# Weight slabs split into four places, and token-tile-major first slabs behind the norms of a two-block transformer kernel

## The chip, the core and the metric

The kernel runs on one core of a Trainium2 chip. The core has the engines PE (TensorE: matmuls), DVE (VectorE), ACT (ScalarE), POOL (GpSimd) and SP (queues transfers), and 16 DMA engines. Each engine runs its own instructions in order and they meet in semaphores. The metric is the device time of one execution in microseconds; lower is better.

## The reference

The input is one sequence of 256 tokens of width 1024, all in float32. The first part has two layers. With `mod = silu(c) @ ada_w[l] + ada_b[l]`, split into six rows (shift, scale and gate for attention and for the FFN), a layer is

```
h = rms_norm(x, norm_g[l, 0]) * (1 + sc_a) + sh_a
x = x + g_a * rms_norm(attention(h), norm_g[l, 1])      # plain causal in layer 0, differential in layer 1
h = rms_norm(x, norm_g[l, 2]) * (1 + sc_f) + sh_f
x = x + g_f * rms_norm((silu(h @ w_gate) * (h @ w_up)) @ w_out, norm_g[l, 3])   # hidden width 2816
```

The second part is a mixer (`w_in`; windowed sums, a short convolution and a linear recurrence; `w_out`), an MLP of hidden width 4096 with a squared relu, a gated projection of a second input `p`, and a final norm.

## The kernel before

**Weights as slabs.** All large weights pass as 145 slabs of 1 MB, in one fixed order: `raw` (128 x 2048 float32) is loaded by SP, ACT rounds it to `w_hi` (`split_hi`, L903), DVE forms the rest `w_lo = raw - w_hi` (`split_lo`, L1238), and PE multiplies with both: `three` (L507 to L509) issues hi*hi, hi*lo and lo*hi. `raw`, `w_hi` and `w_lo` each have RING = 3 places. So `split_hi(n)` waits until PE is done with slab n-3 (`slab_done`), and the load of n waits for `split_lo(n-3)`.

**Kinds of slab.** A column slab (`col_slab`, `v_slab`) holds all 1024 rows and 256 columns of a weight; its 48 matmuls have the weights as the stationary operand and 256 tokens (all of them) as the moving one, or the other way round. A row slab (`row_slab`, `row_last_two`) holds 256 rows and 1024 columns: 24 matmuls with 512 moving columns. Layer l has four head pairs of three column slabs (queries, keys, values), four row slabs of `w_o` (OPROJ), then eleven FFN chunks of two column slabs (gate, up) and one row slab (down). Layer 0 starts at slab 0, its FFN at 16; layer 1 at 49, its FFN at 65. The mixer, the MLP and the gate slabs (PLE_GATE) follow.

**Norms.** Behind the last row slab of attention (b = 0, 2) and of the first FFN (b = 1) the functions `post_norm` on ACT and DVE run over two token tiles of 128: square sums of y, x update, square sums of x, `1/rms`, a diagonal matrix of it (`x_diagonal`, L1311), `turn_normed` on PE (x times that matrix, which turns and scales it, L595, with bf16 `keep_warm` matmuls between), the modulation by gain and shift (`t_modulated`, L1326, all on DVE), `hi_part` (L935) and `lo_part` (L1338). The next `col_slab` needs h of all 256 tokens (`Z_NEED`).

**Modulations.** `ada_w` is 48 loads of 1 MB, each summed by DVE in two steps (`ada`, L1246 and L1250). The first 8 come by SP, 40 by POOL's queue (`load_ada`, L465) through three places of `ada_raw`. In layer 0's attention each head pair consumes three; the four of layer 0's FFN gate (items 20 to 23) come around the first norm, in layer 0's FFN four are consumed per two chunks, and the last four in layer 1's attention. Sums become rows by `spread_row` (float32 matmuls with ones, L580) for `gate_row` and columns by `reduce_mods` and `reduce_tile`.

**Order.** The order on every engine is written out by hand. On ACT and DVE each `split_hi` and `split_lo` has its place between the other steps; in a head pair DVE also does `biased` (L1416 to L1435), `normalised` (L1440 to L1462) and ACT the exponentials (`exps`, L983, L985).

Of the kernel before, what the change touches and what calls it, by code (L numbers as in the profile page):

```python
# [7 lines left out]
F32 = mybir.dt.float32  # L8
# [34 lines left out]
RING = 3  # L43
# [17 lines left out]
SH_A, SC_A, G_A, SH_F, SC_F, G_F = range(6)  # L61
ADA_RING = 3

LATER_MODS = (SH_A, SC_A, SH_F, SC_F, G_A)
# [6 lines left out]
OP_ACC = [sorted({0, 1, 2, 4, 7} - {(a + 3 * PAIRS - 1) % RING}) for a in ATTN]  # L71
# [3 lines left out]
TURN = [[4, 5, 6, 7], [2, 3, 5, 6], [0, 2, 4, 5], [0, 3, 5, 6], [0, 1, 4, 5], [1, 2, 4, 5], [4, 5, 6, 7]]  # L75

WARM = {1: 0, 2: 3, 3: 1}
# [3 lines left out]
Z_NEED = [(2, 4)] + [(3, 4)] * 6  # L81
# [10 lines left out]

class Slab:


    def __init__(self, first, stride=0, i=0):
        self.first, self.stride, self.i = first, stride, i

    def __add__(self, k):
        return Slab(self.first + k, self.stride, self.i)  # L100
# [5 lines left out]
    @property  # L106
    def turn(self):
        return self.first // RING + (self.stride // RING) * self.i if self.stride else self.first // RING

    def plus(self, k):  # L110
        return self.first + k + self.stride * self.i if self.stride else self.first + k
# [22 lines left out]
def build(nc, x, c, rel_bias, ada_w, ada_b, norm_g, moba_w_qkv, moba_w_o, diff_w_qkv, diff_w_o, diff_lambda,  # L134
# [8 lines left out]
    with ExitStack() as ctx:  # L143
# [6 lines left out]
        raw = sb("raw", [P, RING, SLAB])  # L150
        w_hi = sb("w_hi", [P, RING, SLAB], F32R)
        w_lo = sb("w_lo", [P, RING, SLAB], F32R)
        ada_raw = sb("ada_raw", [P, ADA_RING, 2, D])
# [5 lines left out]

        junk_x = sb("junk_x", [P, 2, HALF_D])  # L160
# [10 lines left out]
        bias = sb("bias", [P, HEADS, LINE])  # L171
# [6 lines left out]
        ones_r = sb("ones_r", [P, 2], F32R)  # L178
# [3 lines left out]
        c_pair = sb("c_pair", [P, 2])  # L182
# [32 lines left out]
        junk_y = [t[:].rearrange("p a b -> p (a b)") for t in (silu_g, hid)]  # L215
# [8 lines left out]


# [6 lines left out]
        xb, gate_r, gate_i, a_t, th, mult = (view(n) for n in range(6))  # L232
# [3 lines left out]
        pool_d = bias_flat[:, 2 * CT * S:3 * CT * S].rearrange("p (t s) -> p t s", t=CT)  # L236
# [22 lines left out]
        def h_part(h, t, c):  # L259
            return h[:, 4 * c:4 * c + 4, tokens(t)]  # L260

        slab_loaded = [sem(f"slab_loaded_{i}") for i in range(RING)]
        slab_hi, slab_lo, slab_done = sem("slab_hi"), sem("slab_lo"), sem("slab_done")
        first_mods = [sem(f"first_mods_{i}") for i in range(6)]
# [3 lines left out]
        c_pair_ready = sem("c_pair_ready")  # L268
# [14 lines left out]
        diag_ready, turned, t_ready, hi_ready, h_ready = (  # L283
            sem(n) for n in ("diag_ready", "turned", "t_ready", "hi_ready", "h_ready"))
# [28 lines left out]
        def first_mod_place(m):  # L313

            if 3 <= m < 6:
                return raw[:, m - 3].rearrange("p (k n) -> p k n", k=2), first_mods[m % 6]
            return ada_raw[:, (m + 1) % ADA_RING], first_mods[m % 6]
# [30 lines left out]
        def _(sp):  # L348
            def load(n, src, parts):

                if n.stride or n.first >= RING:
                    sp.wait_ge(slab_lo, n.plus(1 - RING))
                else:
                    sp.wait_ge(ada_acc, 2 * (n.first + 4))
                sp.dma_start(parts(raw[:, n.place]), src).then_inc(slab_loaded[n.place], 16)

            def load_gate_rows(b):
# [3 lines left out]
                sp.wait_ge(h_ready, 4 * (b + 1))  # L361
                if b:
                    sp.wait_ge(y_gained, 4 * b)
# [8 lines left out]
            def first_mod(m):  # L372
                buffer, done = first_mod_place(m)
                if m >= 6:
                    sp.wait_ge(ada_acc, 2 * (m - 5))
                sp.dma_start(buffer, rows(ada_w[0][:, ds(m // 4 * D, D)], m % 4)).then_inc(done, 16)
# [22 lines left out]
            for l in range(DEPTH):  # L399
                for t in range(3):  # L400
                    load(Slab(ATTN[l] + t), cols(w_qkv[l], t * D), as_cols)
                with sp.Fori(1, PAIRS) as j:
                    for t in range(3):
                        load(Slab(ATTN[l] + t, 3, j), cols(w_qkv[l], j * 256 + t * D), as_cols)
                load_gate_rows(2 * l)
                for j in range(KT // 2):
                    load(Slab(OPROJ[l] + j), rows(w_o[l], j), as_rows)
                load(Slab(FFN[l]), cols(ffn_w_in[l], 0), as_cols)
                load(Slab(FFN[l] + 1), cols(ffn_w_in[l], D_FF), as_cols)

                def load_chunk(n, j):
# [3 lines left out]

                with sp.Fori(0, FF_CHUNKS - 3) as j:
                    load_chunk(Slab(FFN[l] + 2, 3, j), j)
                load_gate_rows(2 * l + 1)
                for j in (FF_CHUNKS - 3, FF_CHUNKS - 2):
                    load_chunk(Slab(FFN[l] + 2 + 3 * j), j)  # L420
# [19 lines left out]
            sp.wait_ge(y_gained, 4 * 4)  # L440
            sp.dma_start(grow[:], on_all(norm_final_g_2, 0)).then_inc(final_row_loaded, 16)
            load(Slab(MLP), cols(w_up_2[0], 0), as_cols)
            with sp.Fori(0, (UP_CHUNKS - 1) // 3) as i:
                for c3 in range(3):
                    n = Slab(MLP + 1 + 2 * c3, 6, i)
                    load(n, cols(w_up_2[0], i * 768 + 256 * (c3 + 1)), as_cols)
                    load(n + 1, rows(w_down_2[0], i * 3 + c3), as_rows)
            sp.wait_ge(mix_ready, 2)
# [12 lines left out]
        def _(pool):  # L461
            def load_ada(l, kp, col, place, need):

                pool.wait_ge(ada_acc, need)
                pool.dma_start(ada_raw[:, place], rows(ada_w[l][:, ds(col, D)], kp)).then_inc(ada_loaded[place], 16)  # L465
# [1469 lines left out]
```

## Time and profile before

| | before |
|---|---|
| median of 3 runs | 1021.24 us (1018.68 to 1021.3) |
| the profiled execution's own time | 1020.94 us |
| its span | 1019.2 us |
| PE, DVE, ACT busy | 940.8, 683.6, 471.7 us |
| DMA | 213 MB, 209 GB/s over the span |

The span is the time from the first to the last instruction of the profiled execution. Matmuls are pipelined, so a busy matmul shows a length of its own, and the distance of two starts is what it costs.

### The profile page before, as it was taken

The numbers are of one execution on the slowest core, as the hardware profiler recorded it, in microseconds if no ns is written. First come the engines' busy times: TensorE is split into PE (matmuls) and PEld (weight loads), VectorE is DVE, ScalarE is ACT, GpSimd is POOL, SyncE is SP. The second block draws the span as 40 slices with busy tenths as digits, with TensorE's granted clock in tenths as the row PEclk, the third lists the DMA queues.
The fourth block names the chain that finished last, engine by engine and source line by source line (L and its number), as shares of the span: only waits on it lengthen the run. The fifth ranks groups of instructions, "written<-read, shape, count | busy, mean of one in ns | idle before, by whom it ended". The sixth has DMA issues, their size and how long they took to land.

```text
span 1019.2 us, 15585 instructions
## 1 busy us (share of the span) xinstructions
PE 940.8 (92%) x6301; PEld 861.1 (84%) x6301; DVE 683.6 (67%) x793; ACT 471.7 (46%) x599; POOL 37.3 (4%) x93
## 2 busy tenths in 40 slices
PE   1699998999999989999899999997997999999985
PEld 1699977999999979997789999996986999999864
DVE  5788877968767778887754444456895554555555
ACT  2254445434334345766554343434483544354553
POOL 2101100100000000000000000000000000000000
PEclk9799999999999999999999999998999999999988
DMA  8999960989779645655245556662444656665511
GB/s 336 369 329 325 342 227 36 356 296 338 272 268 364 233 151 165 207 209 170 75 165 176 196 174 214 200 217 92 143 152 139 197 175 193 181 203 187 178 69 41
DMA packets 127840, 213.00 MB, mean 209 GB/s; under 512 B 4673, under 2 KB 97970, under 8 KB 127794
## 3 DMA queue, kind: packets, MB, share of 16 engines
q1 hardware_dynamic: 116466, 168.82, 49.6%
q0 software_dynamic: 11328, 43.53, 11.6%
q8 instruction: 33, 0.54, 0.2%
q14 instruction: 13, 0.11, 0.0%
HBM read 211.28 MB, written 1.06 MB: 208 GB/s over the span
## 4 chain that ended last, share of the span: by engine, by line
PE 79%; DVE 9%; ACT 5%; DMA 4%; issue 2%; SPq 0%; DVEq 0%; ACTq 0%
PE ps L507 25%; PE ps L509 24%; PE ps L508 24%; DMA raw<-in_moba_w_qkv 3%; DVE w_lo L1238 2%; ACT w_hi L903 2%; DMA ada_raw<-in_ada_w 1%; DVE yg L1326 1%; DVE ada_sum L1250 1%; PE ps L694 1%; PE ps L580 1%; PE ps L595 1%; DVE h_lo L1338 1%; DVE yg L1333 1%; ACT h_hi L935 1%
## 5 line engine op out<-in xcount | busy, mean ns | idle before, releaser
L1238 DVE TENSOR_TENSOR w_lo<-raw,w_hi 128x2048 fp32r<-128x2048 f32 x145 | 331.8, 2290 | 202.5 <-ACT w_hi L903 202.3
L903 ACT ACTIVATE w_hi<-raw 128x2048 fp32r<-128x2048 f32 x145 | 276.7, 1910 | 245.3 <-PE ps L509 227.2
L507 PE MATMUL ps<-h_hi,w_hi 128*128 128x256 f32 x1312 | 376.9, 287 | 11.5 <-DVE h_lo L1338 9.7
L508 PE MATMUL ps<-h_lo,w_hi 128*128 128x256 f32 x1312 | 374.5, 285 | 0.0
L509 PE MATMUL ps<-h_hi,w_lo 128*128 128x256 f32 x1312 | 374.3, 285 | 0.0
L507 PEld LDWEIGHTS ps<-h_hi,w_hi 128*128 128x128 f32 x1312 | 255.2, 194 | 15.3 <-issue 11.4
L508 PEld LDWEIGHTS ps<-h_lo,w_hi 128*128 128x128 f32 x1312 | 255.2, 194 | 1.2
L509 PEld LDWEIGHTS ps<-h_hi,w_lo 128*128 128x128 f32 x1312 | 255.1, 194 | 0.0
L507 PE MATMUL ps<-w_hi,o_hi 128*128 128x512 f32 x264 | 106.0, 402 | 4.7 <-issue 1.7
L509 PE MATMUL ps<-w_hi,o_lo 128*128 128x512 f32 x264 | 103.5, 392 | 0.0
L508 PE MATMUL ps<-w_lo,o_hi 128*128 128x512 f32 x264 | 103.5, 392 | 0.0
L1250 DVE SCALAR_TENSOR_TENSOR ada_sum<-ada_raw,c_act,ada_sum 128x1024 f32<-128x1024 f32 x51 | 65.4, 1282 | 4.4 <-DMA ada_raw<-in_ada_w 3.2
L507 PEld LDWEIGHTS ps<-w_hi,o_hi 128*128 128x128 f32 x264 | 50.1, 190 | 15.5 <-issue 3.8
L509 PEld LDWEIGHTS ps<-w_hi,o_lo 128*128 128x128 f32 x264 | 49.8, 189 | 10.9
L508 PEld LDWEIGHTS ps<-w_lo,o_hi 128*128 128x128 f32 x264 | 50.1, 190 | 9.1
L507 PE MATMUL ps<-w_hi,hid_hi 128*128 128x512 f32 x144 | 57.1, 397 | 0.1
L507 PE MATMUL ps<-w_hi,h_hi 128*128 128x256 f32 (+1 forms) x160 | 50.9, 318 | 6.4 <-DVE w_lo L1238 5.4
L508 PE MATMUL ps<-w_lo,hid_hi 128*128 128x512 f32 x144 | 56.2, 390 | 0.0
L509 PE MATMUL ps<-w_hi,hid_lo 128*128 128x512 f32 x144 | 56.0, 389 | 0.0
L508 PE MATMUL ps<-w_lo,h_hi 128*128 128x256 f32 (+1 forms) x160 | 49.8, 311 | 0.0
L509 PE MATMUL ps<-w_hi,h_lo 128*128 128x256 f32 (+1 forms) x160 | 49.6, 310 | 0.0
L1054 ACT ACTIVATE silu_g<-ps 128x512 f32<-128x512 f32 x22 | 13.1, 596 | 78.3 <-PE ps L509 78.3
(241 smaller groups left out, 964.5 us busy)
## 6 DMA issues: line engine op xcount, KB each, us to landing
raw<-in_ffn_w_in SPq DMA_DIRECT2D x44, 1024.0 KB, 5.2
ada_raw<-in_ada_w POOLq DMA_DIRECT2D x40, 1024.0 KB, 7.5
raw<-in_ffn_w_out SPq DMA_DIRECT2D x22, 1024.0 KB, 5.0
raw<-in_w_up SPq DMA_DIRECT2D x16, 1024.0 KB, 5.7
raw<-in_w_down SPq DMA_DIRECT2D x16, 1024.0 KB, 4.9
raw<-in_moba_w_qkv SPq DMA_DIRECT2D x12, 1024.0 KB, 8.5
raw<-in_diff_w_qkv SPq DMA_DIRECT2D x12, 1024.0 KB, 5.2
raw<-in_w_in SPq DMA_DIRECT2D x6, 1024.0 KB, 5.1
```

The costliest lines, as they stand in the source:

```text
L507: T.matmul(out_ap, hi_s, hi_m, start=start, stop=False, skip_group_check=True)
L508: T.matmul(out_ap, hi_s, lo_m, start=False, stop=False, skip_group_check=True)
L509: return T.matmul(out_ap, lo_s, hi_m, start=False, stop=stop, skip_group_check=True)
L580: last = T.matmul(ps[:, banks[c]], ones[:], ada_sum[:, slot, half(c)], start=True, stop=True)
L595: last = T.matmul(ps[:, TURN[z][2 * t + c], f * P:(f + 1) * P], xt[:, t, fs], diag[:, t], start=True, stop=True)
L694: T.matmul(late, q[rs, hh, P:S], k[rs, hh, :], start=True, stop=True)
L903: A.activation(w_hi[:, n.place], raw[:, n.place], ACT.Copy).then_inc(slab_hi, 1)
L935: A.activation(h_part(h_hi, t, c), turned_tile(t, c), ACT.Copy).then_inc(hi_ready, 1)
L1054: A.activation(silu_g[:], ps[:, n.place], ACT.Silu).then_inc(silu_ready, 1)
L1238: V.tensor_tensor(w_lo[:, n.place], raw[:, n.place], w_hi[:, n.place].bitcast(F32), ALU.subtract).then_inc(slab_lo, 1)
L1250: V.scalar_tensor_tensor(out=ada_sum[:, slot], in0=buffer[:, k], scalar=scalars[k], in1=ada_sum[:, slot], op0=ALU.mult, op1=ALU.add)\
L1326: last = V.tensor_scalar(turned_tile(t, c)[:, f], ps[:, TURN[z][2 * t + c], f * P:(f + 1) * P], gains[:, k:k + 1], mods[:, shift, k:k + 1] ...
```

## The change

- `w_hi` and `w_lo` have four places, `raw` keeps three (RAW = 3, RING = 4). `split_hi(n)` waits for the end of slab n-4, and nearly every split on ACT and DVE is of the slab after the one that it was (n+3 for n+2, and so on). PSUM banks go by `first % 3` as before. Room comes from `bias` (256 columns instead of 384), `junk_x` (gone), the third place of `ada_raw` (now `yg`) and views laid over others.
- Behind the three norms with modulation the first two slabs are half-row slabs (`load_two`: 512 rows, 256 columns each of gate and up, or of queries and keys). `first_two` multiplies them token tile by token tile, 512 moving columns at a time. Results have tokens as rows: `hidden_tokens` and `tokens_out` bring them to SBUF, and transposes turn the hidden chunk (4) or queries and keys (8).
- x is scaled by DVE (`xs_ready`) and transposed, instead of multiplied by a diagonal; tile 1's transposes stand within `first_two`. Half of `t_modulated` is on ACT.
- `spread_row` takes sums that are split into hi and lo (`gate_hi`, `gate_lo`), two float32r matmuls for one float32 matmul.
- Items of `ada_w` have a new order (`ADA`): layer 0's FFN gate is summed in layer 0's FFN, five items per two chunks; two of layer 1's attention gate in layer 1's attention; layer 1's FFN gate in its FFN. Places are held until the h of a norm is ready.
- Layer 1's `lambda_and_decay` moves behind the first split of its attention. Loops over chunks and pairs are written out (no `Fori`).

The core of the diff:

```diff
-RING = 3
+RAW = 3
+RING = 4
-LATER_MODS = (SH_A, SC_A, SH_F, SC_F, G_A)
+LATER_MODS = (SH_A, SC_A, SH_F, SC_F)
...
+            def first_two(n, z, banks, turn_second):
+                for t in range(ST):
+                    for s in range(2):
+                        if t == 0:
+                            pe.wait_ge(slab_lo, n.plus(s + 1))
+                        pe.wait_ge(h_ready, 4 * z + 2 * t + s + 1)
+                        wh, wl = as_halves(w_hi[:, (n + s).place]), as_halves(w_lo[:, (n + s).place])
+                        for k in range(4):
+                            if (t, s, k) == (0, 1, 2):
+                                turn_second()
+                            kk = 4 * s + k
+                            last = three(ps[:, banks[t]], h_hi[:, kk, tokens(t)], h_lo[:, kk, tokens(t)],
+                                         wh[:, k], wl[:, k], kk == 0, kk == KT - 1)
+                        if t == 1:
+                            last.then_inc(slab_done, 1)
+                    if t == 0:
+                        last.then_inc(first_done, 1)
...
+                pe.wait_ge(gate_lo_ready, b + 1)
+                hi, lo = gate_split(b)
                 for c in range(2):
-                    last = T.matmul(ps[:, banks[c]], ones[:], ada_sum[:, slot, half(c)], start=True, stop=True)
+                    T.matmul(ps[:, banks[c]], ones_r[:], hi[:, half(c)], start=True, stop=False, skip_group_check=True)
+                    last = T.matmul(ps[:, banks[c]], ones_r[:], lo[:, half(c)], start=False, stop=True,
+                                    skip_group_check=True)
...
+                    if l and first:                                  # PE, first pair of layer 1
+                        first_two(n, 2, QK_TOKENS, lambda: turn_second(2))
+                        v_slab(n + 2, {1: turn_queries_keys, 5: lambda: scores(pairs * 3 + 2)})
+                        return
...
+                    if l and first:                                  # ACT, first pair of layer 1
+                        tokens_out(n, QK_TOKENS, 0)
+                        split_hi(n + 3)
+                        tokens_out(n, QK_TOKENS, 1)
+                        split_hi(n + 4)
+                        act.wait_ge(tok_turned, 2)
+                        queries_out(ps[:, QK_TURNED[0]])
+                        A.activation(qkv[:, 1], ps[:, QK_TURNED[1]], ACT.Copy).then_inc(qkv_out, 1)
+                        values_out(n + 2)
+                        exps(pairs + 1)
+                        split_hi(n + 5)
+                        return
...
+                    if first:                                        # DVE, a head pair
+                        split_lo(n + 2)
+                    if l == 0:
+                        ada(FIRST_MODS + 3 * j)
+                    elif first:
+                        lambda_and_decay()
                     split_lo(n + 3)
+                    if l == 0:
+                        ada(FIRST_MODS + 3 * j + 1)
+                    elif j < 2:
+                        ada(ADA_GA + 2 + j)
+                    if l and first:
+                        split_lo(n + 4)
                     if l:
                         biased(pairs + 1, 2 * j)
...
+                    if l and first:
+                        split_lo(n + 5)
                     normalised(pairs + 1, j + 1)
...
+                gate_lo(2 * l)                                       # DVE, before w_o; gate_hi stands so on ACT
                 split_lo(n + 3)
```

## Rows read from the trace of the kernel before

**Rows 1.** The page: its head and the engines' busy time.

```profile
span 1019.2 us, 15585 instructions
...
PE 940.8 (92%) x6301; PEld 861.1 (84%) x6301; DVE 683.6 (67%) x793; ACT 471.7 (46%) x599; POOL 37.3 (4%) x93
```

**Rows 2.** Timeline of PE, from a row slab to a column slab: start, length.

```profile
542.05 0.39 PE L509 MATMUL ps<-w_hi,hid_lo 128*128 128x512 f32 x1
542.28 0.28 PE L507 MATMUL ps<-h_hi,w_hi 128*128 128x256 f32 x1
...
542.51 0.28 PE L509 MATMUL ps<-h_hi,w_lo 128*128 128x256 f32 x1
```

**Rows 3.** Stretches: length, busy time of each engine, PE's clock, DMA share, GB/s.

```profile
56.00:127.00 71.00, 70.14 (x558) 68.29 (x556) 63.07 (x70) 33.66 (x51) 7.74 (x11) 1.00 0.93 333
...
214.00:362.00 148.00, 147.42 (x1035) 137.59 (x1036) 106.71 (x81) 57.70 (x44) 9.86 (x14) 1.00 0.81 286
...
703.00:720.00 17.00, 10.57 (x61) 9.96 (x60) 11.77 (x24) 10.31 (x20) 0.00 (x0) 0.70 0.11 35
```

**Rows 4.** Groups of instructions: busy us, mean ns, idle time before them.

```profile
L1238 DVE TENSOR_TENSOR w_lo<-raw,w_hi 128x2048 fp32r<-128x2048 f32 x145 | 331.8, 2290 | 202.5 <-ACT w_hi L903 202.3
L903 ACT ACTIVATE w_hi<-raw 128x2048 fp32r<-128x2048 f32 x145 | 276.7, 1910 | 245.3 <-PE ps L509 227.2 <-DMA raw<-in_moba_w_qkv 18.1
...
L1250 DVE SCALAR_TENSOR_TENSOR ada_sum<-ada_raw,c_act,ada_sum 128x1024 f32<-128x1024 f32 x51 | 65.4, 1282 | 4.4 <-DMA ada_raw<-in_ada_w 3.2
...
L1326 DVE TENSOR_SCALAR yg<-ps,gain,mods 128x128 f32<-128x128 f32 x64 | 21.7, 402 | 3.6 <-PE ps L595 3.6
...
L1338 DVE TENSOR_TENSOR h_lo<-yg,h_hi 128x512 fp32r<-128x512 f32 x28 | 19.1, 688 | 7.7 <-ACT h_hi L935 7.1
...
L935 ACT ACTIVATE h_hi<-yg 128x512 fp32r<-128x512 f32 x28 | 17.4, 629 | 54.1 <-DVE yg L1333 29.4 <-DVE yg L1326 24.7
...
L985 ACT ACTIVATE prob<-prob,maxes 128x128 f32<-128x128 f32 x24 | 9.3, 387 | 0.0
```

**Rows 5.** The chain of waits around layer 0's first norm: start, length, what.

```profile
134.93 1.98 PE ps L580 x4
...
159.82 0.91 PE ps L595 x8
...
185.03 0.39 PE ps L507
```

**Rows 6.** The chain of waits at the start of layer 1's attention.

```profile
396.50 0.61 ACT qkv L1023
```

**Rows 7.** Timeline of DVE, ACT and PE in layer 1's first head pair.

```profile
400.09 0.42 DVE L1423 TENSOR_TENSOR prob<-ps,bias 128x256 f32<-128x256 f32 x1
...
404.38 0.51 ACT L983 ACTIVATE prob<-prob,maxes 128x256 f32<-128x256 f32 x1 [5.49 <-DVE maxes L1435]
...
409.58 1.41 DVE L1462 SCALAR_TENSOR_TENSOR prob<-prob,rsums 128x256 f32<-128x256 f32 x4
...
416.13 0.27 PE L646 MATMUL ps<-ident,prob 128*128 128x128 f32 x1
```

**Rows 8.** The chain of waits around layer 1's FFN norm.

```profile
477.78 3.64 PE ps L580 x4
...
499.64 0.91 PE ps L595 x8
...
525.20 0.38 PE ps L507
```

**Rows 9.** PE's waits from 480 to 800 us: us in total, times, longest.

```profile
PE ps L507 <- DVE w_lo L1238: 2.6, 2, 1.5
```

**Rows 10.** Timeline of PE at the gate slabs, the kernel's end.

```profile
987.21 0.79 PE L507 MATMUL ps<-w_hi,h_hi 128*128 128x512 f32 x1 [2.74 <-DVE w_lo L1238]
...
998.53 0.47 PE L507 MATMUL ps<-w_hi,h_hi 128*128 128x512 f32 x1 [2.71 <-DVE w_lo L1238]
```

**Rows 11.** Timeline of ACT at the kernel's start.

```profile
57.36 1.91 ACT L903 ACTIVATE w_hi<-raw 128x2048 fp32r<-128x2048 f32 x1 [0.34 <-DMA raw<-in_moba_w_qkv]
```

More of the change, by code:

```diff
@@ L710, in pair @@
                         turn_heads(j)
-                pair(0, Slab(ATTN[l]), True)
-                with pe.Fori(1, PAIRS) as j:
-                    pair(j, Slab(ATTN[l], 3, j), False)
+                for j in range(PAIRS):
+                    pair(j, Slab(ATTN[l] + 3 * j), j == 0)
                 pairs = PAIRS * (l + 1)
@@ new lines, in _ @@
+                last.then_inc(tok_turned, 1)
+                col_slab(n + 1, None, FF_UP[l])
+                down(n + 2, base + 1, 0)
+                for chunk in range(2, FF_CHUNKS - 1):
+                    n = Slab(FFN[l] + 3 * chunk - 1)
+                    gate_up(n, base + chunk)
+                    if chunk == FF_CHUNKS - 2:
+                        pe.wait_ge(mod_ready, 8)
+                        spread_row((FF_FREE[l], MISC), 2 * l + 1)
+                    turns = l == 0 and chunk % 2 == 0
+                    if turns:
+                        i = chunk // 2 - 1
+                        pe.wait_ge(ada_lo_ready, i + 1)
+                        pe.wait_ge(mod_ready, i + 4)
+                    down(n + 2, base + chunk, (chunk - 1) % 2, reduce_tile if turns else None)
@@ L840, in up_down @@
                 row_slab(n + 1, FF_ACC, hidden_parts(parts), False)
-            with pe.Fori(0, (UP_CHUNKS - 4) // 3) as i:
-                for c3 in range(3):
-                    up_down(Slab(MLP + 1 + 2 * c3, 6, i), i * 3 + (c3 + 1), c3)
+            for chunk in range(UP_CHUNKS - 4):
+                up_down(Slab(MLP + 1 + 2 * chunk), chunk + 1, chunk % 3)
             for o in range(2):
@@ new lines, in _ @@
+                hidden_tokens(1)
+                split_lo(n + 4)
+                dve.wait_ge(hid_hi_ready, base + 1)
+                V.tensor_tensor(hidden_parts(0)[1], ps[:, MISC].rearrange("p (o s) -> p o s", o=2),
+                                hidden_parts(0)[0].bitcast(F32), ALU.subtract).then_inc(hid_lo_ready, 1)
+                for chunk in range(1, FF_CHUNKS):
+                    n = Slab(FFN[l] + 3 * chunk - 1)
+                    last, even = chunk == FF_CHUNKS - 1, chunk % 2 == 0
+                    i = (chunk - 1) // 2
+                    m = ADA_LATER + 5 * i
+                    if last:
+                        gate_row(2 * l + 1, (FF_FREE[l], MISC), (9, 11)[l])
+                    split_lo(n + 3)
+                    if l == 0 and not last:
+                        ada(m + (3 if even else 0))
+                    if l and chunk <= KT // 2:
+                        ada(ADA_GF + chunk - 1)
+                    if not last:
+                        split_lo(n + 4)
+                    if chunk == FF_CHUNKS - 2:
+                        gate_lo(2 * l + 1)
+                    if l == 0 and not last:
@@ L1865, in _ @@
             x_scaled(0)
-            split_lo(n)
+            split_lo(n + 1)
             x_scaled(1)
```

778 lines of the change are left out of this document (384 added, 394 removed).

## The prediction

> **What bounds the kernel now.** I read the page first: PE is busy for 940.8 of 1019.2 us, DVE for 683.6 [rows 1]. A busy matmul overlaps the next, so I took PE's cost from distances of starts: one with 512 moving columns takes 0.23 us, two with 256 take 0.23, so 0.12 each (the finer value is 0.1195) [rows 2]. A row slab of 24 is then 5.5 us, a column slab of 48 is 5.75 us, and 145 slabs are some 820 us. Then the stretches: in layer 0's attention after the start (56 to 127 us) and in its FFN (214 to 362 us) PE is idle for 0.9 and 0.6 us at full clock, with the DMA queues at 333 and 286 GB/s [rows 3]. These stretches, which with the second layer's and the MLP are most of the time, are bound by PE, and an earlier split gives nothing there. ACT's 245 us and DVE's 202 us of idle time before the splits are mostly waits for PE through the three places [rows 4]; they matter only where PE then waits for a split. What is left to win lies between the stretches: the start, the three norms with modulation, the mixer and the gate slabs at the end. I read the chain of waits and PE's timeline there.
>
> **Layer 0's FFN norm.** The last slab of w_o ends at 159.82; PE starts the third FFN slab (the first of the second chunk) at 185.03 [rows 5]. That is 25.2 us, of which the two slabs are 11.5. New order, counted from 159.82: the transposes of tile 0's first half take 0.45 (half of the 0.91 of the eight float32 passes [rows 5]). DVE modulates one quarter in 4 instructions, some 1.4 us at the 0.34 between overlapped starts behind the 402 ns [rows 4]. ACT can start its own quarter 1.2 behind 159.82, after the last square sum. The trace before has no modulation on ACT. Its price: below, four times the 0.29 between starts of a 128-column exponential with one per-partition operand (387 ns long [rows 4]), 1.3 us; above, four times 0.6 (the length of a 512-column h_hi, 629 ns), 2.4 us. It is nearest to the 128-column row, with a second operand that adds some 0.09: I take 1.6. Then two h_hi (0.63, the second 0.53 later) and an h_lo (0.69) [rows 4]: PE starts at +3.9. Twelve matmuls 2.75, six 1.35, tile 1's transposes 0.9 (its x update, square sums, root and two scalings end at about +7.6, in time for them), six more 1.35: +10.3. Tile 1's quarters then take 1.6 + 0.6 + 0.7 behind their transposes at +9.0, so PE waits until +11.9, and 24 matmuls (5.5) end at +17.3. ACT's table load and split of the third slab and DVE's split (1.3 + 1.9 + 2.3) end at the same time. So 17.3 for 25.2, less 0.45 for the four transposes of the hidden chunk: 7.4 us saved.
>
> The row of ones costs 1.98 at 134.93 [rows 5]; four float32r matmuls cost 0.91, and `gate_lo` is ready in time, because ACT and DVE run one slab ahead: 1.0 saved. PE's wait for the biased scores of 0.7 us at 127 goes too, as DVE no longer waits there for w_hi. Against it stands DVE's queue in the first two FFN chunks: five sums of 2.5 us per two chunks instead of four, 6 splits of 2.2, hidden 2 x 1.2 and the split of the column sums 1.2 are 30 of 36.3 us, so the stretch stays PE's, but it begins late: from +19.1 (DVE) split, sum, split, sum, split, sum ... I count `hidden` of chunk 2 at 0.8 us and the split of the sums of the next chunk at 2.0 us after PE wants them; from chunk 4 on the queue has caught up. Loss 2.8 (bounds 0 and 5). Sum for this place: 7.4 + 1.0 + 0.7 - 2.8 = 6.3 us. DMA in this FFN goes from 10 to 11 MB per 36.3 us, 318 GB/s, under the 333 at which the attention stretch kept PE busy [rows 3].
>
> The Trainium skill speaks against this step: "ScalarE: Activation LUTs", section "What ACT_TABLE_LOAD costs", has 186 ns plus 0.833 ns per element and 93 ns for each per-partition operand, overlapped by 93. By it the four modulations are an estimated 1.6 us, and the sum is the same; by the lower bound above it would be 0.6 us per norm better.
>
> **Layer 1's attention (second norm).** PE's part is as above: the first two slabs end some 7 us earlier than now, when the last key left ACT at 397.1 [rows 6], and queries and keys are turned inside the value slab. But DVE's order behind them is split, `lambda_and_decay` 3.3, split, sum 2.5, split, and only then `biased`: it starts at about 399.5 against 400.09 now [rows 7], one split more ahead of it than before. From its start 4.3 to the exponentials (404.38), 3.5 more for them [rows 7]; then ACT splits slab n+5 (1.9), DVE splits it (2.3 [rows 4]) and only then normalises (2.9, ending now at 411.0 [rows 7]). Ready: 399.5 + 4.3 + 3.5 + 1.9 + 2.3 + 2.9 = 414.4. PE has finished the next queries and keys by 409 (now at 416.13 [rows 7]) and turns the probabilities only then: a stall of some 5.4 us takes the place of the one removed. A stall of 2.74 us before the end was followed by a spell at half clock: 24 matmuls that take 5.5 took 8.6 [rows 10]. I put 2 us for it here. Gain of this place 7 - 5.4 - 2 = 0 (bounds -3 and +7: if DVE got through earlier, all of it stays). The row of ones in chunk 9 gives 0.7.
>
> **Layer 1's FFN norm.** As layer 0's, 499.64 to 525.20 now, 25.6 us [rows 8]. Here ACT and DVE must do two splits between the last head and the norm, where one stood: DVE enters the norm 2.7 us later, of which 2.2 reach PE. `gate_lo` stands behind the normalisation and a split, at 480.0, while PE is ready at 477.78; the four matmuls then take 1.8 at half clock instead of 3.64 [rows 8]: 0.4 lost. So 25.6 - 17.3 - 0.45 - 2.2 - 0.4 = 5.2 saved, and 0.8 for the row of ones in that FFN: 6.0.
>
> **Mixer.** PE waited twice for a split between 480 and 800 us, 2.6 us in all, 1.5 at the last two slabs of w_out [rows 9]. That split now stands ahead of the recurrence's last steps: 1.5 saved.
>
> **Gate slabs.** PE waits 2.74 and 2.71 us for splits [rows 10], the second slab runs 3.1 us slow. With one more slab split ahead the second slab's halves are there at 972, and the last two at 991.35, while PE arrives at 990.0. PE's last 11.2 us start at 991.4 instead of 998.53: 7.1 saved. The work behind it is the same.
>
> **Start.** Keys now leave ACT behind the split of slab 4, which before came after them, at 57.36 and waiting for its load [rows 11]. Its load competes with 1.5 MB less from POOL's queue (bias 1.0 for 1.5 MB, the third sum's load held back). I take a loss of 0.7 (bounds -2 and +2). Loops written out, the missing copies of `c_pair`, and `clear_acc` cost or give nothing: PE shows no gap at a loop's turn, and the clear lay in a wait. If instruction fetch lost this cover, it would be the pauses of a rival, not of the sum.
>
> **Sum.** 6.3 + 0.7 + 6.0 + 1.5 + 7.1 - 0.7 = 20.9 us. The profiled execution took 1020.94 us (span 1019.2), 0.3 under the median of 1021.24: 1000.0 us. A measurement tells 0.3%, some 3 us, from no change.
>
> **Rivals.**
> - *No stall in layer 1's first pair.* For it: biased scores may start sooner, each of the five steps is short. Against: all are in DVE's written order. Gives 7 more: 993. Chance 0.17.
> - *The clock falls at each norm.* PE's transposes replace products with a diagonal, and only 8 keep-warm matmuls are left. For it: in the fourth norm, which turns by transposes and has a 5 us wait, the stretch 703 to 720 has a clock of 0.70 [rows 3]. Against: the new waits of PE are under 2 us. A half-clock slab costs 2.5 to 3 us, three times: 1008. The skill's "TensorE: Matmul & The Clock Gate", Part 4, says that transposes do not count as busy for the clock, which would bring this about; no row before parts transposes from waits. Chance 0.15.
> - *The end gives nothing*, as the load of the last slabs or ACT becomes late: 7.1 less, 1007. Against: these loads have 10 us of room. Chance 0.07.
> - *Slower: layer 0's FFN is bound by the sums.* The fifth load per two chunks comes late, and DVE waits in order, with splits behind it. It decides from 4.7 us per two chunks over 4.5 such periods (21 us), that is, if 11.5 MB take 41 us, 280 GB/s. 286 GB/s took a share of 0.81 [rows 3], so some 350 are to be had. At 43 us the result is 1030. Chance 0.06.
> - *No change worth measuring*: new waits in the norms (ACT's share of the modulation at 2.4 us, DVE late) eat all: 1019. Chance 0.05.
>
> **How the numbers follow.** The forecast has the remaining 0.50, with its own range of 994 to 1006. Faster by over 0.3%: 0.50 + 0.17 + 0.15 + 0.07 = 0.89, same 0.05, slower 0.06. The range 987 to 1010 takes in the first three rivals with their bounds and leaves out the last two and a little below.
>
> **What would show it.** Right: third FFN slab 17 to 18 us behind the last of w_o in both layers; PE idle for 4 to 6 us before the turned probabilities of layer 1's first pair; one wait of 1.4 us instead of two of 2.7 at the gate slabs; DVE waited for in chunks 2 and 3 of layer 0. Wrong: waits for sums in every FFN period, clock under 1 behind each norm, or no stall in layer 1.

## The result and the profile after

The changed kernel takes 1013.17 us (median of 5, 1012.85 to 1014.3) against 1021.24 us (median of 5, 1018.68 to 1023.44): a ratio of 0.9925, 95% interval 0.9912 to 0.9938. It is 8.1 us faster, where 21 were forecast; 1013.17 lies above the range. The profiled execution took 1013.14 us with a span of 1011.3. The head of its page and the engines' busy time, to be held against [rows 1]:

```profile
span 1011.3 us, 14324 instructions
...
PE 919.6 (91%) x6067; PEld 842.1 (83%) x6071; DVE 682.3 (67%) x775; ACT 484.7 (48%) x631; POOL 36.3 (4%) x92
```

PE is busy for 21.2 us less, and the span is 7.9 shorter, so PE's idle time has grown by 13 us; the question is where. The stretches, with the same columns as [rows 3]:

```profile
127.00:160.00 33.00, 32.10 (x164) 27.30 (x163) 21.08 (x31) 15.56 (x28) 0.00 (x0) 0.95 0.60 192
...
178.00:214.00 36.00, 33.51 (x243) 31.38 (x242) 30.58 (x22) 17.07 (x14) 3.51 (x5) 1.00 0.93 337
214.00:362.00 148.00, 139.68 (x983) 130.91 (x982) 109.67 (x88) 55.66 (x42) 11.91 (x17) 0.98 0.86 303
```

Layer 0's FFN, where PE was idle for 0.6 of 148 us [rows 3], now has 8.3 us of idle time. The prediction had called that stretch bound by PE and had expected a gain of 0.7 there. PE's waits of the changed kernel say who is waited for (us in total, times, longest):

```profile
PE ps L682 <- DVE yg L1463: 22.3, 2, 20.2
PE ps L566 <- DVE h_lo L1482: 16.5, 9, 5.8
PE ps L664 <- DVE o_lo L1407: 8.0, 2, 7.7
PE ps L734 <- DVE prob L1635: 5.9, 2, 5.0
...
PE ps L664 <- DVE h_lo L1407: 3.2, 1, 3.2
...
PE ps L782 <- ACT qkv L1183: 2.0, 1, 2.0
```

L682 are the transposes, L664 is the first matmul of the row of ones, L734 turns the probabilities, L782 are the scores. The third and the fifth are new; the fourth was 0.9 us in all before, the last 1.4 in two places.

To see what each part was worth I took the same landmark in both timelines of PE (the start of a given slab, or for w_o its end) and subtracted. A term is the difference of two neighbouring landmarks' lags.

| place | from, to (before; after) | gain | forecast |
|---|---|---|---|
| start to the first scores | 57.07; 59.22 | -2.15 | -0.7 |
| attention of layer 0, its row of ones | to the transposes at 159.66; 160.02 | +1.79 | +1.7 |
| first norm | to the third FFN slab, 185.03; 177.73 | +7.66 | +7.4 |
| first FFN chunks | to the third chunk, 221.35; 216.93 | -2.88 | -2.8 |
| chunks 3 to 8 | to 330.19; 325.82 | -0.05 | 0 |
| row of ones in the ninth chunk | to 348.98; 353.32 | -8.71 | +0.7 |
| second norm | to the slab behind the value slab, 404.61; 402.06 | +6.89 | +7 |
| layer 1's first pair | to the first slab of w_o, 469.38; 474.18 | -7.35 | -7 |
| row of ones, layer 1's attention | to the end of w_o, 499.64; 505.84 | -1.40 | -0.4 |
| third norm | to the third FFN slab, 525.20; 525.92 | +5.48 | +5.6 |
| layer 1's FFN | to 679.85; 680.60 | -0.03 | +0.8 |
| mixer and MLP | to the gate slabs, 978.79; 977.89 | +1.65 | +1.5 |
| gate slabs | to the last two, 998.53; 990.60 | +7.03 | +7.1 |

The gains sum to 7.9, the forecasts to 20.9. (In layer 1's first pair the prediction's own terms, 5.4 and 2, make 7.4; its sum took 7. It booked the transposes of the hidden chunk, 0.45, with the norms; they stand behind that landmark, so in the table 0.35 us of them falls to the row below the first and the third norm.) One term, the row of ones in the ninth chunk, carries 9.4 of the 13.0 us between them; the start 1.5, the row of ones in layer 1's attention 1.0, layer 1's FFN 0.8.

**The place that failed.** Timelines of the changed kernel around it, first SP's DMA issues (start, length):

```profile
305.65 0.37 SPq L411 DMA_DIRECT2D raw<-in_ffn_w_out  x1
325.20 0.34 SPq L428 DMA_DIRECT2D grow<-in_norm_g  x1
325.58 0.43 SPq L429 DMA_DIRECT2D yg<-in_ada_b  x1
326.44 1.01 SPq L411 DMA_DIRECT2D raw<-in_ffn_w_in  x2
```

Then the chain of waits through it (start, length, what):

```profile
326.44 9.15 DMA raw<-in_ffn_w_in
...
335.61 1.92 ACT w_hi L1003
...
337.56 2.29 DVE w_lo L1382
...
343.95 1.23 DVE o_lo L1407
...
345.32 0.77 PE ps L664
```

From 305.65 to 325.20, 19.5 us, SP issues nothing. In its written order it stands at the loads of the gate row for the FFN. One of them goes into `bias_row`, which is `yg[:, 0]`, and the change made `yg` the third buffer for the modulations' parts; so `load_gate_rows` got a wait for the sums (`sp.wait_ge(ada_acc, 2 * 40)` for this row). That sum ends at 325.1 on DVE. Three slab loads stand behind the row in SP's queue and start at 326.4 where the first could have started at some 311. ACT waits 14.8 us for the first of them, and `gate_lo` stands on DVE behind that slab's split, a sum and the next split, although its own input has long been there. PE is ready for the row of ones at 337.58 and gets it at 345.32, and the matmuls behind it start at half clock: the clock of 338 to 352 is 0.76.

**The places that held.** The chain through the first norm, with the columns of [rows 5]:

```profile
160.21 0.70 ACT hid L1010 x2
...
161.20 1.49 ACT yg L1045 x4
162.68 0.53 ACT h_hi L1039
163.23 0.70 DVE h_lo L1482
...
168.44 0.89 PE ps L682 x8
169.35 1.50 ACT yg L1045 x4
170.86 0.53 ACT h_hi L1039
171.41 0.70 DVE h_lo L1482
```

ACT's modulation of a quarter takes 1.50 us (forecast 1.6). PE starts at 164.07, 3.9 us behind the last slab of w_o, and at 177.73 the third slab runs. The gate slabs of PE, against the two waits of [rows 10]:

```profile
977.89 0.47 PE L566 MATMUL ps<-w_hi,h_hi 128*128 128x512 f32 x1 [0.95 <-DVE h_lo L1482]
990.60 0.47 PE L566 MATMUL ps<-w_hi,h_hi 128*128 128x512 f32 x1 [1.58 <-DVE w_lo L1382]
```

And the stall that was forecast in layer 1's first head pair, on DVE, ACT and PE, against [rows 7]:

```profile
411.52 3.70 ACT L1003 ACTIVATE w_hi<-raw 128x2048 fp32r<-128x2048 f32 x2
...
417.40 0.58 ACT L1183 ACTIVATE qkv<-ps 128x512 f32<-128x512 f32 x1
```

```profile
413.45 2.29 DVE L1382 TENSOR_TENSOR w_lo<-raw,w_hi 128x2048 fp32r<-128x2048 f32 x1 [5.49 <-ACT w_hi L1003]
...
417.20 1.41 DVE L1635 SCALAR_TENSOR_TENSOR prob<-prob,rsums 128x256 f32<-128x256 f32 x4
```

```profile
418.75 0.45 PE L734 MATMUL ps<-ident,prob 128*128 128x128 f32 x1 [5.01 <-DVE prob L1635]
```

### The profile page after: what moved, and what is told of

Read it like the earlier page. It is cut to its first block, busy times and chain, and to the rows that moved or that the text cites. A ratio compares the mean times of both kernels' runs of the same rounds, so it can differ in the third digit from the quotient of the medians.

```text
span 1011.3 us, 14324 instructions
## 1 busy us (share of the span) xinstructions
PE 919.6 (91%) x6067; PEld 842.1 (83%) x6071; DVE 682.3 (67%) x775; ACT 484.7 (48%) x631; POOL 36.3 (4%) x92
## 4 chain that ended last, share of the span: by engine, by line
PE 76%; DVE 11%; ACT 5%; issue 3%; DMA 3%; SPq 0%; DVEq 0%; ACTq 0%
PE ps L566 24%; PE ps L568 23%; PE ps L567 23%; DVE w_lo L1382 3%; DVE ada_sum L1400 3%; ACT w_hi L1003 2%; DMA ada_raw<-in_ada_w 1%; DVE h_lo L1482 1%; PE ps L782 1%; DMA raw<-in_ffn_w_in 1%; DMA raw<-in_moba_w_qkv 1%; ACT yg L1045 1%; PE ps L655 1%; ACT h_hi L1039 1%; DVE yg L1477 1%
## 5 line engine op out<-in xcount | busy, mean ns | idle before, releaser
L566 PE MATMUL ps<-h_hi,w_hi 128*128 128x256 f32 x1216 | 348.4, 287 | 10.3 <-DVE h_lo L1482 8.6
L567 PE MATMUL ps<-h_lo,w_hi 128*128 128x256 f32 x1216 | 346.5, 285 | 0.0
L568 PE MATMUL ps<-h_hi,w_lo 128*128 128x256 f32 x1216 | 346.5, 285 | 0.0
L566 PEld LDWEIGHTS ps<-h_hi,w_hi 128*128 128x128 f32 x1216 | 236.0, 194 | 13.2 <-issue 9.4
L567 PEld LDWEIGHTS ps<-h_lo,w_hi 128*128 128x128 f32 x1216 | 236.1, 194 | 1.2
L568 PEld LDWEIGHTS ps<-h_hi,w_lo 128*128 128x128 f32 x1216 | 235.8, 194 | 0.0
L566 PE MATMUL ps<-w_hi,h_hi 128*128 128x256 f32 (+1 forms) x208 | 69.3, 333 | 9.5 <-DVE h_lo L1482 7.9
L567 PE MATMUL ps<-w_lo,h_hi 128*128 128x256 f32 (+1 forms) x208 | 67.4, 324 | 0.0
L568 PE MATMUL ps<-w_hi,h_lo 128*128 128x256 f32 (+1 forms) x208 | 67.4, 324 | 0.0
L566 PEld LDWEIGHTS ps<-w_hi,h_hi 128*128 128x128 f32 x208 | 39.6, 190 | 15.9 <-issue 7.1
```

The source lines that it names most:

```text
L566: T.matmul(out_ap, hi_s, hi_m, start=start, stop=False, skip_group_check=True)
L567: T.matmul(out_ap, hi_s, lo_m, start=False, stop=False, skip_group_check=True)
L568: return T.matmul(out_ap, lo_s, hi_m, start=False, stop=stop, skip_group_check=True)
```

## The experiments

Each run below is the changed kernel with one edit unless it says otherwise. The median is given, and the span of its profiled execution, which compares with 1011.3. Executions whose edit acts only later reach the third FFN slab up to 1.7 us later than the changed kernel's 177.73, so the verdict on an edit is read from its own stretch of PE's timeline.

**e1_rows_later: the gate row's loads one chunk later in SP's queue.**

```diff
-                    if j == FF_CHUNKS - 3:
+                    if j == FF_CHUNKS - 2:
                         load_gate_rows(2 * l + 1)
```

> The changed kernel with one step of SP's queue moved: the loads of the FFN gate row (norm weights and bias row) stand behind the loads of the last but one chunk instead of one chunk earlier; nothing else. Theory A (SP's queue): in the changed kernel these loads wait for the last sum of layer 0 (ended 325.04), because the bias row goes into the buffer that the third sum's loads use, and the three slab loads behind them start at 326.44 instead of some 311; ACT waits 14.8 us for the first of them, gate_lo stands behind that slab's split on DVE, and PE waits 7.74 us. Moved, the slab loads start at about 311, the wait of PE is gone and the stretch from the ninth chunk's first slab to the tenth's falls from 27.5 to about 18 us: 9.5 us less, 1003.7. Theory B (DVE is simply full in this FFN, with five sums per two chunks): the wait only moves to the next splits, under 3 us less, 1010 or more. Theory C (the load itself, 9.15 us where the usual one is 5.4, is slow from contention with POOL's loads): 3 to 4 us less.

1004.48 us (1003.9 to 1005.06), span 1003.3, against the kernel before 0.9834 (0.9799 to 0.9870). SP's issues in this run:

```profile
312.46 6.54 SPq L411 DMA_DIRECT2D raw<-in_ffn_w_in  x2
323.97 0.37 SPq L411 DMA_DIRECT2D raw<-in_ffn_w_out  x1
326.55 0.34 SPq L428 DMA_DIRECT2D grow<-in_norm_g  x1
326.94 0.43 SPq L429 DMA_DIRECT2D yg<-in_ada_b  x1
```

The slab loads go out from 312.5, the gate row's at 326.5, much as before, where nothing urgent stands behind them. The ninth chunk takes 18.5 us instead of 27.5 (327.1 to 345.6), 9.0 less, and PE's wait there is 0.28. (The kernel before needs 18.8, so with the loads out of the way the row of ones gives 0.3 here, not the 0.7 that was forecast.) Theory A holds; DVE has room for its five sums, and the load is not slow by itself.

**e2_ones_ahead: SP's queue as it is, gate_hi and gate_lo ahead of the late splits.**

```diff
-                    split_hi(n + 3)
                     if chunk == FF_CHUNKS - 2:
                         gate_hi(2 * l + 1)
+                    split_hi(n + 3)
...
+                    if chunk == FF_CHUNKS - 2:
+                        gate_lo(2 * l + 1)
                     split_lo(n + 3)
...
-                    if chunk == FF_CHUNKS - 2:
-                        gate_lo(2 * l + 1)
```

> The changed kernel with SP's queue as it is, but in the chunk before the last the two parts of the gate row (gate_hi on ACT, gate_lo on DVE) stand ahead of the splits of that chunk instead of behind them; in both layers. Theory A: slab loads still start at 326.4, but PE no longer waits for gate_lo at 337.6; it does the row of ones and the row slab that is long split until about 344, when the late slabs 29 and 30 are split (339.8 and 344.0). The wait of 7.7 us goes down to at most 2: 6 to 8 us less, 1006. Theory B (the late loads themselves are what PE waits for, wherever gate_lo stands): at most 2 us less, 1011.

1008.92 us (1007.04 to 1013.98), span 1007.5. The row of ones runs at 339.02 without a wait, and then PE waits for `hidden`, which DVE has behind the late splits too:

```profile
348.86 0.58 PE L566 MATMUL ps<-h_hi,w_hi 128*128 128x256 f32 x1 [3.30 <-DVE hid L1720]
```

The ninth chunk takes 21.5 us (327.4 to 348.9), 6.0 less than 27.5. So with the loads late, 6 of the 9 us come through the place of `gate_lo` behind the late split and 3 through what else stands behind it. In the span 3.8 us of it show: this execution is 1.6 us behind already at its third FFN slab, and some 0.7 more are lost behind the tenth chunk's start.

**e3_before_rows_wait: the kernel before, with the wait alone.**

```diff
                 sp.wait_ge(h_ready, 4 * (b + 1))
+                if b == 1:
+                    sp.wait_ge(ada_acc, 2 * 40)
```

> The kernel before with only the wait added: its loads of layer 0's FFN gate row wait for the sum number 40 (the last of chunk 8, ended 318.07). Three slab loads behind them start some 13 us later than now (318 instead of 305). Theory A (a wait in SP's queue costs what the late split then holds up, and here no part of the row of ones stands behind a split): the first late slab is needed at 330.2 and would be split at about 331.5: 1 to 3 us more, 1023. Theory B (the wait alone costs what it cost the changed kernel): 8 to 10 us more, 1030.

1035.89 us (1033.04 to 1037.39), span 1031.3 against 1019.2: 12 us longer in the span, and by the ratio, 1.0149 (1.0112 to 1.0186) of the kernel before, 15 us. From the eighth chunk's first slab to the ninth's PE needs 34.9 us instead of 19.2: the loss in its own stretch is 15.7 us, of which the span shows less, because this execution was 1.7 us ahead at the first norm and wins 2 back in layer 1. Theory A was wrong, and the loss is above B's upper bound. ACT's timeline, and then DVE's and PE's:

```profile
328.99 1.91 ACT L905 ACTIVATE w_hi<-raw 128x2048 fp32r<-128x2048 f32 x1 [13.14 <-DMA raw<-in_ffn_w_in]
```

```profile
330.93 2.29 DVE L1240 TENSOR_TENSOR w_lo<-raw,w_hi 128x2048 fp32r<-128x2048 f32 x1 [14.61 <-ACT w_hi L905]
333.14 1.22 DVE L1597 TENSOR_TENSOR o_lo<-ada_sum,o_hi 128x1024 fp32r<-128x1024 f32 x1
```

```profile
334.41 0.79 PE L509 MATMUL ps<-w_hi,o_hi 128*128 128x512 f32 x1 [13.44 <-DVE o_lo L1597]
```

I had asked when PE needs the late slab (330) and not what stands behind its split on ACT and DVE. `hidden` and the split of the column sums stand there, and PE wants them at 321. A load that is late by 13 us cost 13.44 us of PE's time, though the slab itself had 9 us of room. A late load is late for everything that is written behind its split.

**e4_norm_keys_first and e7_norm_first: the order in layer 1's first pair.** The first has both halves of this edit, the second only DVE's:

```diff
-                    split_hi(n + 3)
+                    if l == 0 or j != 1:
+                        split_hi(n + 3)
                     act.wait_ge(slab_done, n.plus(1))
                     queries_out(ps[:, n.bank])
-                    split_hi(n + 4)
+                    if l == 0 or j != 1:
+                        split_hi(n + 4)
                     act.wait_ge(slab_done, n.plus(2))
                     A.activation(qkv[:, 1], ps[:, (n + 1).bank], ACT.Copy).then_inc(qkv_out, 1)
+                    if l and j == 1:
+                        split_hi(n + 3)
+                        split_hi(n + 4)
...
+                    normalised(pairs + 1, j + 1)
                     if l and first:
                         split_lo(n + 5)
-                    normalised(pairs + 1, j + 1)
```

> The changed kernel; in layer 1's first head pair DVE normalises the probabilities ahead of the split of the slab behind, and in the second pair ACT copies queries and keys out ahead of its two splits. Theory A (the stall of 5.0 us at 418.7 is the split of 2.3 and ACT's split of 1.9 ahead of the normalisation, and then the copies of the keys at 417.4): PE turns the probabilities at about 414.5, the scores follow at 415.2 instead of 420.19: 5 us less, 1008. Theory B (the stall is the biased scores' late start at 403.7, so the order behind the exponentials changes little): under 1.5 us less, 1012.

> Only half of the run before it in layer 1's first pair: DVE normalises ahead of the split, ACT's order stays. Theory A (two waits in a row: probabilities, then keys): the probabilities are turned at 414.5, but the scores wait for ACT's copy of the keys, which ends at 418.0: 2 us less, 1011. Theory B (DVE's order is all of it): as much as both together, 3.7 us less in the span.

Both: 1009.83 us (1009.34 to 1015.86), span 1007.6. DVE's order alone: 1013.28 us (1010.44 to 1016.35), span 1011.5. From the last matmuls of the first pair's value slab to the slabs of the third pair PE needs 30.4 us in the changed kernel, 26.4 with both and 29.6 with DVE's half. PE with both, and with one half:

```profile
414.79 0.30 PE L734 MATMUL ps<-ident,prob 128*128 128x128 f32 x1 [1.01 <-DVE prob L1640]
```

```profile
415.86 0.33 PE L734 MATMUL ps<-ident,prob 128*128 128x128 f32 x1 [2.02 <-ACT qkv L1154]
...
418.14 1.23 PE L782 MATMUL ps<-qkv 64*128 64x256 f32 x4 [1.41 <-ACT qkv L1183]
```

The stall was two waits in one place, DVE's normalisation and ACT's copies of queries and keys behind two splits. Taking one away shows the other: 0.9 us gained (2 were expected; the scores do start 2.05 earlier, but they and the heads' matmuls behind them take 5.6 us instead of 4.6, more of it at half clock). Both together give 4.0 of the 5 expected; PE now waits 1.6 us between the scores and the heads' matmuls.

**e5_late_tail: the gate slabs' splits one step later.** `split_hi` and `split_lo` of the four gate slabs stand at the kernel before's places. This is DVE's part; ACT's is the same with `split_hi`:

```diff
-            split_lo(n + 4)
             dve.wait_ge(p_hi_ready, 1)
...
             x_scaled(0)
-            split_lo(n + 1)
+            split_lo(n)
             x_scaled(1)
...
-            split_lo(n + 2)
+            split_lo(n + 1)
             dve.wait_ge(x_rms, 10)
             V.reciprocal(rsx[:, 6], rmsx[:, 6]).then_inc(x_rstd, 1)
-            split_lo(n + 3)
+            split_lo(n + 2)
...
+                if j == 0:
+                    split_lo(n + 3)
```

> The changed kernel with the splits of the four gate slabs one step later on ACT and DVE, at the places that they have in the kernel before (the last of them behind the first scaled gate); four places stay. Theory A (the 7.0 us of the kernel's end come from the one slab of lead): the two waits of 2.7 us and the half-clock slab come back: 7 us more, 1020. Theory B (they come from something else, such as the earlier loads or the four places themselves): no change, 1013.

1022.76 us (1020.64 to 1026.14), span 1022.0. PE's gate slabs:

```profile
989.24 0.50 PE L566 MATMUL ps<-w_hi,h_hi 128*128 128x512 f32 x1 [2.72 <-DVE w_lo L1383]
...
999.67 0.47 PE L566 MATMUL ps<-w_hi,h_hi 128*128 128x512 f32 x1 [3.07 <-DVE w_lo L1383]
```

The waits of 2.7 us are back, and from the first gate slab to the last PE needs 31.6 us instead of 23.8: 7.8 us for 7 expected. The lead of one slab is what the end gained from. (Of the other 2.9 us of the span 1.7 came in the first 200 us and 0.6 around the ninth chunk.)

**e6_whole_tile: PE waits for the whole of h behind all three norms.**

```diff
+                turn_second()
+                pe.wait_ge(h_ready, 4 * z + 4)
                 for t in range(ST):
                     for s in range(2):
                         if t == 0:
                             pe.wait_ge(slab_lo, n.plus(s + 1))
-                        pe.wait_ge(h_ready, 4 * z + 2 * t + s + 1)
...
-                            if (t, s, k) == (0, 1, 2):
-                                turn_second()
```

> The changed kernel, but PE turns tile 1 before it starts tile 0 of the two half-row slabs and waits for all four quarters of h before the first product, behind all three norms; everything else as it is (modulation halved with ACT, split a slab ahead). Theory A (the gain of 7.5 us at each norm is the overlap of tile 0's products with tile 1's chain): PE starts the two slabs at +11.9 instead of +3.9 and needs 11 us: third slab at +23 instead of +17.7, 5.3 us more at each of three norms, and more where PE's longer idle time is followed by half clock: 1029 to 1035. Theory B (the gain is mostly the halved modulation and the earlier splits): under 2 us at each norm, 1013 to 1019.

1032.75 us (1031.43 to 1034.34), span 1032.4. PE's two waits at the first norm (start, length):

```profile
168.83 1.97 PE L681 MATMUL ps<-ident,yg 128*128 128x128 f32 x8 [4.39 <-DVE yg L1462]
174.24 0.79 PE L566 MATMUL ps<-w_hi,h_hi 128*128 128x512 f32 x1 [3.44 <-DVE h_lo L1481]
```

From the first transpose to the third FFN slab PE needs 25.2 us (161.68 to 186.87) instead of 17.7: 7.5 more where 5.3 were expected, as the two slabs take 12.6 for 11 behind the waits, part of it at half clock. The kernel before needed 25.4 between the same two places. The stretches of the other two norms are 8.1 and 8.0 longer, and layer 1's first pair 3.8 shorter, since DVE has caught up there by the time PE comes. So the gain at a norm is the overlap of tile 0's products with tile 1's chain; where PE waits for all of h, the halved modulation, the transposes for diagonal products and the earlier splits together give 0.2 us.

**e8_start_keys: in layer 0's first pair the keys ahead of the split of slab 4.**

```diff
-                    split_hi(n + 4)
+                    if not (l == 0 and first):
+                        split_hi(n + 4)
                     act.wait_ge(slab_done, n.plus(2))
                     A.activation(qkv[:, 1], ps[:, (n + 1).bank], ACT.Copy).then_inc(qkv_out, 1)
+                    if l == 0 and first:
+                        split_hi(n + 4)
```

> The changed kernel; in layer 0's first pair ACT copies the keys out ahead of the split of slab 4, as the kernel before does. Theory A (PE's wait of 2.05 us for the keys at 59.2 is that split, which waited 4.05 us for its load): the scores start at about 57.9: 1.3 to 2 us less, 1011.5. Theory B (the whole start is late by its loads, and the next wait takes it over): no change.

1013.02 us (1011.77 to 1014.76), span 1011.2: no change. The scores start at 57.99 instead of 59.22, and the lead of 1.2 us holds up to 195.0 (196.2 in the changed kernel). At the next chunk it is gone (216.8 against 216.9), and PE's wait there for the split of the column sums is 2.7 us instead of 1.6. DVE's timeline shows why:

```profile
203.45 2.60 DVE L1403 SCALAR_TENSOR_TENSOR ada_sum<-ada_raw,c_act,ada_sum 128x1024 f32<-128x1024 f32 x2 [0.96 <-DMA ada_raw<-in_ada_w]
```

Between 190 and 220 us the DMA share is 1.0 in both runs: the restarted slab loads and the sums' loads fill the queues. So in this execution theory B holds. It is no rule, though: the combined kernel below has the same edit, comes to this FFN 2.5 us earlier than the changed kernel, has no such wait of DVE, and still has the whole 2.5 us at the third chunk (214.47 for 216.93). Why the load came late in e8 stays open, and so whether the edit is worth 0 or 1.2 us.

**e9_gate_lo_first: in layer 1's attention gate_lo one split earlier.**

```diff
                         heads_low(pairs, heads_before)
+                    if l and j == PAIRS - 1:
+                        gate_lo(2)
                     if not (l and first):
                         split_lo(n + 5)
...
-                gate_lo(2 * l)
+                if l == 0:
+                    gate_lo(0)
                 split_lo(n + 3)
```

> The changed kernel; in layer 1 DVE computes gate_lo for the attention's gate row ahead of the last pair's fifth split instead of behind it. Theory A (PE's wait of 3.21 us at 484.89 and the half clock behind it are that one split of 2.3): gate_lo ends at about 482.5, when the turned probabilities are copied out too, so PE starts the row of ones there: 2.3 us less, and up to 1 more where the clock then stays: 1010.5. Theory B (the late split only moves the wait to the row slabs behind): under 1 us less.

1011.11 us (1010.52 to 1011.32), span 1008.7. PE:

```profile
483.77 0.47 PE L664 MATMUL ps<-h_hi,ones_r 128*128 128x512 f32 x1 [1.01 <-DVE h_lo L1407]
```

The wait falls from 3.21 to 1.01 us, and the four matmuls take their full-clock distance of 0.23 instead of 0.43. The stretch to the FFN's second chunk is 3.9 us shorter (86.8 for 90.7), 2.2 of them the wait and most of the rest time at full clock.

**e10_combined: e1, e4, e8 and e9 in one kernel.** Its diff is theirs.

> All that helped in one kernel: gate row loads later in SP's queue (8.0 less in the span by itself), normalisation and key copies first in layer 1 (3.7), keys ahead of the split of slab 4 in layer 0 (0 to 1.2), gate_lo ahead of the split in layer 1's last pair (2.3 expected). Theory A (the waits are separate stretches, so they add): 8.0 + 3.7 + 2.3 = 14 less, 999. Theory B (what one frees the next wait takes, as the gain at the start was taken up in layer 0's FFN): 10 less, 1003.

994.94 us (993.76 to 997.0, 5 runs), span 991.9; against the kernel before 0.9746 (0.9721 to 0.9771). The span is 19.4 us under the changed kernel's (the medians are 18.2 apart), more than either theory gave. By stretches: ninth chunk 9.0, first pair 4.0, layer 1's row of ones and norm 3.8, which are what each edit gave in its own stretch and add to 16.8, so the waits add, as in theory A; and 2.5 ahead of layer 0's FFN, where its timeline is at 193.7 instead of 196.2. Of these 0.9 are the keys; 1.4 lie where the last two slabs of w_o run:

```profile
127.00:160.00 33.00, 32.05 (x171) 26.70 (x170) 22.54 (x36) 16.82 (x31) 0.00 (x0) 1.00 0.57 192
```

Its clock there is 1.00, where the changed kernel had 0.95 and needed 12.6 us for these two slabs instead of 11.2. Each of the four edits alone left them at 12.6 to 12.8. But e3, whose only edit first acts some 150 us later, took 11.2 there too, where the kernel before has 12.6. So these 1.4 us come and go between executions, and nothing here shows that the four edits together bring them.

## Why the prediction was wrong

The direction and most of its steps were right; the time was not, by 13 us, and one missed wait is over two thirds of that.

- **Row of ones in the ninth chunk of layer 0** ("The row of ones in chunk 9 gives 0.7", "from chunk 4 on the queue has caught up"; measured -8.7). This is the step that failed. The part on this FFN followed DVE's queue and summed up the DMA, and did not read SP's queue past the moved sums: the gate row's loads now wait for the last of them, with three slab loads behind. e1 moves the loads and has 9.0 us back; e2 leaves them and has 6.0 back by taking `gate_lo` out from behind the late split; e3 puts the wait alone into the kernel before and loses 15.7 us in its stretch, 12 in the span. The term was also too large by itself: without the late loads the row of ones gives 0.3 here.
- **Slower rival: layer 0's FFN bound by the sums.** Its pattern was right (a late load, and DVE in order behind it), its mechanism was not: it was one wait in SP's queue of slab loads, 8.7 us, not a period that repeats; from chunk 3 to chunk 8 the changed kernel loses 0.05 us on the one before.
- **Norms** (7.4, 7 and 5.6 forecast; 7.7, 6.9 and 5.5 measured). The chain was right step by step, and e6 shows that it is the overlap that pays: without it the stretch is back at 25.2 us. The third FFN slab starts 17.6 us behind the last of w_o in layer 0, as the forecast's sign has it, but 20.1 behind it in layer 1: the sign left out the 2.2 us by which DVE comes late to that norm, which the sum had; PE waits 2.13 us for it. The Trainium skill's page "ScalarE: Activation LUTs", section "What ACT_TABLE_LOAD costs", gave an estimated 1.6 us for the four modulations; the trace has 1.50.
- **First FFN chunks** (2.8 forecast, 2.9 measured). The waits are where they were forecast, 0.9 us for `hidden` and 1.6 for the split of the column sums. That DVE's order alone sets them was only argued: in e8 a sum waits 0.96 us for its load there, with the DMA share at 1.0.
- **Layer 1's first pair** (stall of 5.4 and 2 of clock forecast; 5.01 measured, 7.35 in all). Right, and incomplete: ACT's copies of queries and keys were the second wait in the same place, which e7 uncovers.
- **Row of ones in layer 1's attention** (0.4 lost forecast, 1.4 measured). `gate_lo` is where it was reckoned (done at 484.75, that is 479.95 on the clock of the kernel before, for "480.0"), and the row of ones costs 0.5 more than before. What was left out are the heads' matmuls behind it, which run at half clock too, 0.9 us. e9 takes 2.2 us of wait away and gains 3.9.
- **Layer 1's FFN** (0.8 forecast, nothing measured). From the last matmul ahead of the row of ones to the slab behind it PE takes 7.0 us (673.58 to 680.60) where it took 7.3 (672.53 to 679.85): 0.3 gained, as in layer 0 without the late loads, because the float32 row of ones costs 1.32 us between starts here (672.65 to 673.97), less than the 1.98 that were read at 134.93. The transposes of the hidden chunk, 0.35, stand in this stretch and take it back.
- **Start** (0.7 lost forecast, 2.15 measured, beyond the bound of 2). The keys wait behind slab 4's split as forecast, with a wait of 2.05 us where there was one of 0.69: ACT waited 4.05 us for that slab's load. The first slab also starts 1.1 later (43.26 for 42.12): the last sum ends 0.9 later, as DVE scales x ahead of it, two times 0.88 us, where it made two diagonals of 0.29, and PE's reduction behind that sum takes 3.54 us for 2.45. Whether the 1.2 us of the keys would have counted in the end is open: e8 paid them back, the combined kernel did not.
- **Gate slabs** (7.1 and 7.0) and **mixer** (1.5 and 1.65) were right; e5 has 7.8 for the first.
- **The clock at each norm.** This rival did not come: the clock from 160 to 178 us is 1.00 (0.91 before), although PE transposes there, and in the second norm (375.9 to 394) it is 1.00 too. In the third (505.8 to 526) it is 0.92, behind the wait of 2.13 us, where the kernel before has 0.93 (499.6 to 525.2). The Trainium skill's page "TensorE: Matmul & The Clock Gate", Part 4, which says that transposes do not count as busy in the same way, is not contradicted by it, as products and keep-warm matmuls stand between them.

## What to carry to other kernels

When a buffer gets a second user, look for every queue in which a wait is written for it, and list what stands behind that wait; a DMA queue counts as one, and here one wait in it cost more than anything else in the change. A late load is late for all that stands behind its split in the order of the splitting engines, so its room is not the time until its own slab is needed but the time until the first of these is. And where two engines feed one place, an experiment that moves only one of them can show nothing while both together pay.

## What the runs showed of the hardware

Layer 0's last two slabs of w_o, which stand behind the 16 one-column float32 matmuls (32 in the trace) that reduce the modulations, took 12.6 to 12.8 us in seven of the twelve profiled executions, 13.7 to 13.9 in three (e2, e5, e6) and 11.2 in two (e3, e10), with the same instructions: part of them at half clock, by an amount that changes. Such spells are why an edit's worth of 1 or 2 us could be read only from its own stretch. A wait of PE of 3.21 us in layer 1 was followed by 3.4 us at half clock (the four matmuls of 512 columns started 0.43 apart); after a wait of 1.01 us in the same place (e9) they started 0.23 apart. The length of the wait alone does not decide it: at the end of the kernel before, the matmuls behind a wait of 2.74 us started 0.43 apart for 5.6 us, and those behind one of 2.71 us 0.23 apart from the second on.
